# Row tiles of the first four experts: 32-row tiles (four abreast) replaced by 64-row tiles (two abreast)

## The reference

```python
logits = einsum('btd,de->bte', x, w_router)
top_val, top_idx = top_k(logits, 2)
gate = sum(one_hot(top_idx, 8) * softmax(top_val)[..., None], -2)
for e in range(8):
    out = out + gate[..., e:e+1] * swiglu(x, w_gu[e], w_down[e], 3584)
# swiglu: h = x @ w_gu;  (silu(h[..., :3584]) * h[..., 3584:]) @ w_down
```

## Time and profile before

| | us |
|---|---|
| median of the runs | 1730.22 |
| the profiled execution | 1730.22 |
| its span, first to last instruction | 1728.6 |
| TensorE busy, matmuls | 1625.6 |
| VectorE, ScalarE busy | 1041.6, 785.5 |
| DMA over the span | 460.65 MB, mean 266 GB/s |
| mean granted TensorE clock, share of full speed | 0.969 |

### The profile page before, as it was taken

The page is one execution under the profiler, slowest core; times in us unless marked ns, Lnnn a source line. Parts: engine busy times, 40 slices in busy tenths (PEclk is TensorE's granted clock), DMA queues, the critical chain, the costliest instruction groups (busy, mean ns, idle before and its releaser), DMA issues.

```text
span 1728.6 us, 27022 instructions
## 1 busy us (share of the span) xinstructions
PE 1625.6 (94%) x10366; PEld 1242.1 (72%) x10366; DVE 1041.6 (60%) x1356; ACT 785.5 (45%) x949; POOL 103.2 (6%) x187
## 2 busy tenths in 40 slices
PE   8999999999999999999899989787899999999897
PEld 6997899998976666865344535454688888888685
DVE  4998755446745554573213313231788888888797
ACT  4645543325533222342213312221677777777575
POOL 0000000000030541020000000000000000000300
PEclk9999999999998999999999999887999999999999
DMA  8773365442340441039999999999999999999992
GB/s 231 241 217 94 111 168 147 152 142 85 128 138 7 141 136 56 2 143 410 404 397 404 404 406 399 404 403 388 410 405 366 392 376 358 400 371 366 391 372 94
DMA packets 229947, 460.65 MB, mean 266 GB/s; under 512 B 24565, under 2 KB 120468, under 8 KB 229825
## 3 DMA queue, kind: packets, MB, share of 16 engines
q1 hardware_dynamic: 217246, 426.81, 67.5%
q10 hardware_dynamic: 5587, 17.16, 2.8%
q0 software_dynamic: 7008, 15.25, 2.7%
HBM read 440.86 MB, written 18.76 MB: 266 GB/s over the span
## 4 chain that ended last, share of the span: by engine, by line
PE 76%; DMA 9%; DVE 6%; ACT 5%; issue 2%; SPq 1%; POOL 0%; POOLq 0%; ACTq 0%; DVEq 0%
PE ps L2646 9%; PE ps L2802 8%; PE ps L2803 8%; PE ps L2804 8%; PE ps L2117 7%; PE ps L2119 7%; PE ps L2118 7%; DMA raw<-in_moe_w_gu 6%; PE ps L2199 3%; PE ps L2639 3%; PE ps L2640 2%; PE ps L2641 2%; PE ps L2488 2%; DMA raw<-in_moe_w_down 2%; PE ps L2451 2%
## 5 line engine op out<-in xcount | busy, mean ns | idle before, releaser
L1968 DVE TENSOR_TENSOR w_lo<-raw,w_hi 128x2048 fp32r<-128x2048 f32 x168 | 383.7, 2291 | 63.0 <-ACT w_hi L1275 62.1
L1275 ACT ACTIVATE w_hi<-raw 128x2048 fp32r<-128x2048 f32 x168 | 322.4, 1920 | 135.5 <-PE ps L2804 119.5
L1974 DVE TENSOR_TENSOR w_lo<-raw,w_hi 128x2048 fp32r<-128x2048 f32 x42 | 96.3, 2292 | 229.0 <-ACT w_hi L1282 229.0
L2117 PE MATMUL ps<-x_hi,w_hi 128*128 128x304 f32 x672 | 207.9, 309 | 2.2 <-DVE x_lo L1520 1.6
L2119 PE MATMUL ps<-x_lo,w_hi 128*128 128x304 f32 x672 | 202.8, 302 | 0.0
L2118 PE MATMUL ps<-x_hi,w_lo 128*128 128x304 f32 x672 | 202.0, 301 | 0.0
L2802 PE MATMUL ps<-w_hi,g_hi 128*128 128x512 f32 x448 | 177.7, 397 | 11.7 <-DVE w_lo L1968 11.7
L1410 DVE TENSOR_TENSOR w_lo<-raw,w_hi 128x2048 fp32r<-128x2048 f32 (+4 forms) x129 | 135.5, 1096 | 69.7 <-ACT w_hi L1002 69.5
L2803 PE MATMUL ps<-w_lo,g_hi 128*128 128x512 f32 x448 | 176.1, 393 | 0.0
L2804 PE MATMUL ps<-w_hi,g_lo 128*128 128x512 f32 x448 | 176.1, 393 | 0.0
L2646 PE MATMUL ps<-raw,g_s 128*32 128x128 f32 (+3 forms) x1920 | 161.1, 377 | 8.4 <-DMA raw<-in_moe_w_gu 8.4
(11 more groups left out here) (460 smaller groups left out, 2594.3 us busy)
## 6 DMA issues: line engine op xcount, KB each, us to landing
raw<-in_moe_w_gu SPq DMA_DIRECT2D x224, 1024.0 KB, 9.8
raw<-in_moe_w_down SPq DMA_DIRECT2D x112, 1024.0 KB, 9.2
raw<-in_ffn_w_gu SPq DMA_DIRECT2D x44, 512.0 KB, 5.1
raw<-in_conv_w_in SPq DMA_DIRECT2D x16, 512.0 KB, 7.8
raw<-in_ffn_w_down SPq DMA_DIRECT2D x16, 512.0 KB, 4.0
kvn<-in_cache_ckv POOLq DMA_DIRECT2D x64, 128.0 KB, 3.4
kvn<-in_cache_ckv SPq DMA_DIRECT2D x64, 128.0 KB, 2.8
rows_in<-zrow ACTq DMA_DIRECT2D x13, 512.0 KB, 3.7
```

The lines of the kernel that those rows point to most:

```text
L1275: nc.scalar.activation(w_hi[:, u % SPLIT], raw[:, u % RAW], ACT.Copy).then_inc(hi_done, 1)
L1968: V.tensor_tensor(w_lo[:, u % SPLIT], raw[:, u % RAW], w_hi[:, u % SPLIT].bitcast(F32), ALU.subtract).then_inc(lo_done, 1)
L1974: V.tensor_tensor(w_lo[:, n % F_SPLIT], first_raw(k), w_hi[:, n % F_SPLIT].bitcast(F32), ALU.subtract).then_inc(lo_done, 1)
L2117: nc.tensor.matmul(out, hi, xh, start=start, stop=False, skip_group_check=True)
```

## The change

C and H's further rows get 64 rows each, as A and B have: every plain product has two tiles. The table of rows goes away, and `HALF` (64) stands everywhere. With it go these sizes: a tile of C and H has twice the columns, C's and H's turns have more transposes (4 instead of 2 for a step of C, 2 instead of 1 for H's further rows), ScalarE and VectorE work on twice the width there, and the gather has 384 columns instead of 320. The routing arithmetic is simpler by one instruction, one of the DMAs that clear rows at the start falls away, and POOL stores C's and H's rows with 2 DMAs each instead of 4. H's limit is 192 tokens instead of 160 and C's 64 instead of 32 before an expert needs another job.

```diff
-ROWS = {"A": HALF, "B": HALF, "C": HALF // 2, "H": HALF // 2}
-TILES = {x: SLOTS // n for x, n in ROWS.items()}
-PLAIN = sum(ROWS.values())
-PLACES = SLOTS + PLAIN
+PLACES = SLOTS + FIRST_JOBS * HALF
...
-    hT_x = mo("hT_x", [P, SLOTS])
+    hT_x = mo("hT_x", [P, 2, SLOTS])
...
-    g_s = gx("g_s", [P, DC, PLAIN])
-    sgx = gx("sgx", [P, SLOTS])
+    g_s = gx("g_s", [P, FIRST_JOBS, DC, HALF])
+    sgx = gx("sgx", [P, 256])
...
-            for a in range(TILES[x]):
-                pool.dma_start(rows_out[r0:r0 + n, w * a:w * a + w], y_s[x][n * a:n * a + n]).then_inc(f_st, 16)
+            for a in range(2):
+                pool.dma_start(rows_out[r0:r0 + HALF, 512 * a:512 * a + 512], y_s[x][HALF * a:HALF * a + HALF]).then_inc(f_st, 16)
...
-        def plain_tiles(x, bank, n, rows, w, c0, start, stop):
-            for a in range(TILES[x]):
-                m = nc.tensor.matmul(ps[ROWS[x] * a:ROWS[x] * a + ROWS[x], bank, 0:n], rows, w[:, c0 + n * a:c0 + n * a + n],
+        def plain_pair(out, x, w, start, stop):
+            for a in range(2):
+                m = nc.tensor.matmul(out(a), x, w(a), start=start, stop=stop, skip_group_check=True)
...
-                m = nc.tensor.transpose(ps[:, 3, 0:P], hhx[:], ident[:])
+                for c in range(2):
+                    m = nc.tensor.transpose(ps[:, 3, P * c:P * c + P], hhx[:, P * c:P * c + P], ident[:])
...
-                    plain_tiles("H", 1 if kind == "gate" else 3, SLOTS, token_rows("H", c), w, 512 * q, c == 0, c == DC - 1)
+                    plain_pair(half_rows(1 if kind == "gate" else 3, 256), g_s[:, len(SMALL), c], columns(w, 512 * q, 256), c == 0, c == DC - 1)
```

More of the change, by code:

```diff
@@ L419, in build @@
     ADD_AFTER = {12: (0,), 19: (1,), 25: (2,), JOB_UNITS - 2: (3, 4, 5)}
-    y_s = {x: xt[:, i % 3, 512 * (i // 3):512 * (i // 3) + D // TILES[x]] for i, x in enumerate(FIRST_ROWS)}
+    y_s = {x: xt[:, i % 3, 512 * (i // 3):512 * (i // 3) + 512] for i, x in enumerate(FIRST_ROWS)}
     stat = place("stat", A0 + 4 * KB, [P, 3, 4])
@@ L955, in _ @@
             pool.wait_ge(f_fl, FLUSHED[x] + 1)
[L956 to L958 removed]
+            r0 = SLOTS + HALF * FIRST_ROWS.index(x)
+            for a in range(2):
+                pool.dma_start(rows_out[r0:r0 + HALF, 512 * a:512 * a + 512], y_s[x][HALF * a:HALF * a + HALF]).then_inc(f_st, 16)
         nc.gpsimd.iota(slot_no[:], pattern=[[1, SLOTS]], base=0, channel_multiplier=0,
                        allow_small_or_imprecise_dtypes=True).then_inc(slot_made, 1)
[L961 removed]
+        pool.wait_ge(f_st, 2 * FIRST_JOBS * 16)
         pool.wait_ge(last_dve, 3 + 1)
@@ L1322, in _ @@
                 act.wait_ge(unit_used, U_MOE + e + 1)
-                nc.scalar.activation(y_s[x], ps[:, 6 if x == "H" else 7, 0:D // TILES[x]], ACT.Copy).then_inc(f_fl, 1)
+                nc.scalar.activation(y_s[x], ps[:, 6 if x == "H" else 7, :], ACT.Copy).then_inc(f_fl, 1)
             for ahead in (2, 3) if k == 0 else (3,):
@@ L1888, in _ @@
         counts = ps[:, 4, 3 * NEXP:4 * NEXP]
-        key, rank_e, heavy, light, fewer, over, more, plain, dyn, first_row, limit_, shift = [ex[:, i] for i in range(12)]
+        key, rank_e, heavy, light, sign, over, more, plain, dyn, first_row, limit_, shift = [ex[:, i] for i in range(12)]
         square, by_first, tokens = [P, NEXP, NEXP], [P, FIRST_JOBS, NEXP], [P, 3, NEXP]
@@ L1897, in _ @@
         mark(V.tensor_tensor(picked[:], picked[:], eidx[:].unsqueeze(1).broadcast_to(by_first), ALU.mult))
-        chain(V.scalar_tensor_tensor(out=fewer, in0=light, scalar=-float(HALF / ROWS["H"]), in1=heavy, op0=ALU.mult, op1=ALU.add))
+        chain(V.tensor_tensor(sign, heavy, light, ALU.subtract))
         mark(V.reduce_sum(first_f[:], picked[:], AX))
-        chain(V.scalar_tensor_tensor(out=fewer, in0=rank_e, scalar=float(NEXP - 1), in1=fewer, op0=ALU.is_equal, op1=ALU.subtract))
+        mark(V.scalar_tensor_tensor(out=over, in0=sign, scalar=-float(HALF), in1=counts, op0=ALU.mult, op1=ALU.add))
+        chain(V.tensor_scalar(plain, sign, 0.0, None, ALU.is_equal))
         V.tensor_copy(first_i[:], first_f[:]).then_inc(ranked, 1)
-        mark(V.scalar_tensor_tensor(out=over, in0=fewer, scalar=float(ROWS["H"]), in1=counts, op0=ALU.mult, op1=ALU.add))
-        chain(V.tensor_scalar(plain, fewer, 0.0, None, ALU.is_equal))
         mark(V.tensor_scalar(more, over, float(2 * SLOTS), None, ALU.is_gt))
         mark(V.scalar_tensor_tensor(out=first_row, in0=rank_e, scalar=-float(NEXP - len(SMALL)), in1=light, op0=ALU.add, op1=ALU.mult))
-        chain(V.tensor_scalar(limit_, fewer, -float(ROWS["H"]), float(SLOTS), ALU.mult, ALU.add))
+        chain(V.tensor_scalar(limit_, sign, float(HALF), float(SLOTS), ALU.mult, ALU.add))
         mark(V.scalar_tensor_tensor(out=jobs[:], in0=over, scalar=float(SLOTS), in1=more, op0=ALU.is_gt, op1=ALU.add))
-        mark(V.scalar_tensor_tensor(out=first_row, in0=heavy, scalar=FIRST_ROW["H"] / HALF, in1=first_row, op0=ALU.mult, op1=ALU.add))
+        mark(V.scalar_tensor_tensor(out=first_row, in0=heavy, scalar=float(len(SMALL)), in1=first_row, op0=ALU.mult, op1=ALU.add))
         chain(V.scalar_tensor_tensor(out=key, in0=plain, scalar=float(4 * T), in1=limit_, op0=ALU.mult, op1=ALU.add))
@@ L1959, in gathered_lower @@
             of = ps[:, GATHER_LO[c % 3]]
-            V.tensor_copy(g_lo[:, c], of[:, PLAIN:PLACES])
+            V.tensor_copy(g_lo[:, c], of[:, FIRST_JOBS * HALF:PLACES])
             v.wait_ge(f_gh, c + 1)
-            V.tensor_tensor(g_s[:, c], of[:, 0:PLAIN], g_s[:, c], ALU.add).then_inc(f_gl, 1)
+            V.tensor_tensor(g_s[:, :, c], of[:, 0:FIRST_JOBS * HALF].rearrange("p (x n) -> p x n", x=FIRST_JOBS), g_s[:, :, c], ALU.add).then_inc(f_gl, 1)
         def split_moe(k, j):
@@ L2686, in _, with half_rows, columns @@
         gather(3)
-        def token_rows(x, c):
-            return g_s[:, c, FIRST_ROW[x]:FIRST_ROW[x] + ROWS[x]]
+        def half_rows(bank, n):
+            return lambda a: ps[HALF * a:HALF * a + HALF, bank, 0:n]
+        def columns(w, c0, n):
+            return lambda a: w[:, c0 + n * a:c0 + n * a + n]
         def turn_first(x, s):
@@ L2696, in turn_first @@
                     nc.tensor.transpose(ps[:, 2, P * c:P * c + P], hh[:, P * c:P * c + P], ident[:])
-                m = nc.tensor.transpose(ps[:, 3, 0:P], hhx[:], ident[:])
+                for c in range(2):
+                    m = nc.tensor.transpose(ps[:, 3, P * c:P * c + P], hhx[:, P * c:P * c + P], ident[:])
             else:
                 pe.wait_ge(f_hp, SMALL_N[x, s] + 1)
-                for c in range(narrow(x, s) // P):
+                for c in range(narrow(s) // P):
                     m = nc.tensor.transpose(ps[:, 2, P * c:P * c + P], hh_p[:, P * c:P * c + P], ident[:])
@@ L2710, in large_unit @@
                     c = 2 * part + q
-                    plain_tiles("H", 6, D // TILES["H"], hT_x[:, ROWS["H"] * c:ROWS["H"] * c + ROWS["H"]], w, WIDE * q,
-                                s == 0 and c == 0, s == 2 * STEPS - 2 and c == 3)
+                    at = HALF * (c // 2)
+                    plain_pair(half_rows(6, 512), hT_x[:, c % 2, at:at + HALF], columns(w, WIDE * q, 512),
+                               s == 0 and c == 0, s == 2 * STEPS - 2 and c == 3)
                 else:
@@ L2735, in small_unit @@
                     c = 2 * part + q
-                    a, at = divmod(c, narrow(x, s) // P)
-                    m = plain_tiles(x, 7, D // TILES[x], hT_s[:, at, ROWS[x] * a:ROWS[x] * a + ROWS[x]], w, WIDE * q,
-                                    s == 0 and c == 0, s == STEPS - 1 and c == 4 * n - 1)
+                    at = HALF * (c // (2 * n))
+                    m = plain_pair(half_rows(7, 512), hT_s[:, c % (2 * n), at:at + HALF], columns(w, WIDE * q, 512),
+                                   s == 0 and c == 0, s == STEPS - 1 and c == 4 * n - 1)
             else:
@@ L2741, in small_unit @@
                     c = (4 // n) * part + q
-                    m = plain_tiles(x, 0 if kind == "gate" else 2, narrow(x, s), token_rows(x, c), w, 512 * n * q, c == 0, c == DC - 1)
+                    m = plain_pair(half_rows(0 if kind == "gate" else 2, 256 * n), g_s[:, SMALL.index(x), c], columns(w, 512 * n * q, 256 * n),
+                                   c == 0, c == DC - 1)
             return m
```

31 lines of the change are left out of this document (14 added, 17 removed).

## The result

The changed kernel takes 1752.88 us, median of 4 runs (1751.49 to 1755.90), against 1730.06 (1727.85 to 1733.55) for the kernel before in the same comparison: a ratio of 1.0141, 95% interval 1.0127 to 1.0155. It is slower by 22.8 us. 1743 was forecast, with a range to 1751; the direction was right, the size was not. The profiled execution took 1749.95 us, 2.9 less than the median, the least of all executions of this kernel on record; its span is 1748.3 us, 19.7 longer than before, and 19.6 of it stand at the loop's first matmul. So a time read from the traces shows some 3 us less than the medians do.

What follows compares the result with a forecast made beforehand. Weight arrival bound the first four experts; TensorE would take over, 70.6 us added against 60 of slack. The loop would start at 1234 instead of 1220, plus 14, less 1 of gains: 1743 us, range 1733 to 1751.

Steps and rivals of the forecast that it cites:

- end of unit 160: Where the six places of the last units begin, ahead of the loop; forecast to move from about 1198.5 to 1212.5 us.
- work, with the turns' own waits: TensorE's work up to the end of unit 160: 368 us before plus 70.6 added, 438.6 us.
- further waits: TensorE's remaining wait for weights up to the end of unit 160, all at unit 52: 1.4 us.
- from there to the loop: From the end of unit 160 to the loop's start: DMA's path, not the changed work, 21.4 us as before.
- small gains: Unpriced gains, no passage between two tile shapes and a clock that falls less: 1 us taken off.
- Prices of a unit of C, of H's plain part: TensorE time: a unit of C gains 0.87 us over 0.865; H's plain part goes from 1.01 to 1.87.
- 5 of the 18 have no unit to cover the multiplication and take some 1.0 more: Turns up to unit 160: 0.8 us each, five uncovered ones some 1.0 more, 19 us together.
- Later TensorE is behind the arrivals everywhere, so nothing else waits: After unit 52, weights arrive before TensorE needs them, at units 97 and 122 by some 3 and 5 us.
- The wait at unit 52: H's gate after a long run of small units: weights at about 918.5, TensorE at 917.1, 1.4 us of wait.
- Slack as one sum of 60 us: TensorE's work of 368 us in 427.5 before the change leaves 60 us, set against 70.6 added.
- two bounds that add up: Rival: late places idle DMA, then TensorE waits for late weights; 1 to 2 us more per round, 1750 to 1756; chance 0.14.
- The rivals of the other side: Added work hides in the slack, 1731 to 1733, chance 0.10; or full clock makes it faster, 1727, chance 0.04.

Runs made afterwards that it cites:

- a_light: Changed kernel with the weight DMAs of the small experts' units from unit 16 on cut to half their columns: 1729.82 us, ratio 1.0002.
- a_turn: Changed kernel with VectorE's multiplication of hidden rows put ahead of the split of H's next unit at units 26, 98, 122: 1740.57 us, ratio 1.0079.
- h_only: Changed kernel with C back in 32-row tiles, four abreast, the gather keeping 384 columns: 1746.30 us, ratio 1.0095.
- h_turn: Changed kernel with C back in 32-row tiles and the three multiplications put ahead of the split: 1737.56 us, ratio 1.0042.
- b_turn: Kernel before the change, with the same three multiplications put ahead of the split: 1729.81 us, ratio 1.0007.

## Why the prediction was wrong

By its own steps, at the end of unit 160:

| step | forecast | measured |
|---|---|---|
| start of unit 0 | 772.5 | 770.5 |
| work, with the turns' own waits | 438.6 | 432.4 (a_light) |
| further waits | 1.4 | 16.1 |
| end of unit 160 | 1212.5 | 1219.0 |
| from there to the loop | 21.4 | 20.5 |
| loop's first matmul | 1234 | 1239.5 |

The loop is 5.5 us later than forecast. The median missed by 9.9: 1 of it was taken off for small gains, and some 3 lie between the profiled execution and the median.

- *What bounds the kernel, and that TensorE takes over*: right. The loop's rounds did not change, and what the loop starts late by, the end is late by.
- *Prices of a unit of C, of H's plain part*: right to 0.06 us. The sum was 6 us too high. Rows account for some 5: the 0.1 us of the passage from 64-row to 32-row tiles, seen at 21 places, is in the 438.6; a gather group takes 0.91 us and not 1.00; H's plain part in a down unit takes 1.81 and not 1.87; and each small unit was taken some 0.015 too dear. Unit 0 was taken 2 us too late: the first gather matmul starts at 761.77 instead of 763.45, and why was not tested. These two errors hid a part of the other by luck: with them right, the forecast would have been some 1735 and further off.
- *"5 of the 18 have no unit to cover the multiplication and take some 1.0 more"*: this is the step that failed. Two of the five (H's first and third step) do wait 1.1. The other three, A1, B2 and C0, stand ahead of a unit of H and wait in VectorE's queue for that unit: 5.62, 5.51 and 2.49 us, with a slow start behind the first two. Beyond the 2.4 us that they stand in a_light, that is 14.3 of the 16.1 us. The trace of before had it: unit 97 starts at 1027.33 and its turn at 1034.87.

```profile
1027.33 1.94 PE L2646 MATMUL ps<-raw,g_s 128*64 128x512 f32 x8 [0.66 <-DMA raw<-in_moe_w_gu]
1034.87 1.11 PE L2701 MATMUL ps<-ident,hh_p 128*128 128x128 f32 x4 [5.60 <-DVE hh_p L2004]
```

  I read the 7.5 us as part of the 60 us of slack, weights that come late, and took them away with it. But the arrival that the queue waits for moves with TensorE. Unit 26 (its DMA begun at 826.62 before and at 831.80 after) landed at 841.60 and at 844.76, 3.2 us later, and the up unit ahead of A1's turn started 3.2 us later too (838.92, 842.09). At B2 both are some 10 us later (unit 98 landed at 1029.98 and then at 1040.06), and the wait is again 5.5. At C0 TensorE is some 15 us later and unit 122 only 11.5 (1094.51, 1105.99), and there the wait did shrink, from 6.06 to 2.49. a_turn shows what the three cost: 12.3 us by the medians, 10.4 in the traces.
- *"Later TensorE is behind the arrivals everywhere, so nothing else waits"*: wrong in the same way. It compared arrivals as they were before, shifted by 4 us. But DMA can only be as early as places come free: unit 98 landed at 1040.06, not at some 1034.
- *The wait at unit 52*: 1.4 us forecast, 1.4 measured (from its start, 917.43, to the next unit's, 923.64, are 6.21 us against 4.82). That it agrees is in part luck: the wait for `w_lo` is 1.05 of it, 0.20 is the next unit's wait for the turned rows, and both TensorE and the weights came some 2 us later than forecast.
- *Slack as one sum of 60 us*: h_only shows that it isn't one. The time that DMA loses in the first three quarters isn't made good by TensorE's idle time in the last. The rival "two bounds that add up" had a part of this mechanism, late places, and the time, 1750 to 1756, with a chance of 0.14. That its time fits is in part luck, since the queued turns, over half of the cost, were not in it; its own argument against itself, that a swing of 5 us is small against 21 us of places, left out their standstill, which comes on top of the swing.
- *The rivals of the other side*: a unit of C costs double (1.715 against 0.865), and the work did not hide. The clock was full from 1120 to 1220, as foreseen, and fell at two of the turns; no gain came of it.

Of the 22.8 us, a_turn accounts for 12.3. What remains with the turns moved is 11.2 against the kernel before of that comparison, and splits by kernels into 8.0 for H alone (h_turn) and 3 for C on top of it. TensorE's work alone doesn't account for it: with light DMAs (a_light) the changed kernel's loop starts at 1219.4, where the kernel before has 1219.96. In h_turn it is the late start of the DMA stream (in the kernel after unit 9 is issued at 787.53 instead of 785.77) and the thin stretch from 900 to 1000 us, 3.8 and 7.2 us at 402 GB/s, less 2.5 won elsewhere. Which wait makes that second stretch thin, the alternation in H's steps or the turn and unit 52 within it, stays open.

## What to carry to other kernels

Before counting idle time as slack, ask of each wait what it hangs on, and whether that moves when the engine falls behind. Here the data did: its DMA was issued when the engine freed a place, so the two largest waits in the queue, for another unit's work, stayed at 5.5 us with TensorE 3 and 10 us later. Such a wait is free while another engine or DMA is the bound (b_turn), and becomes a cost when its own engine is (a_turn). Slack of one engine also couldn't be pooled over the stretch: what DMA lost early for want of a place was not made good later. Where a kernel alternates work by a fixed order, look for short work for the critical engine that stands behind long work waiting for an arrival, and put it ahead. It cost nothing here, and in the kernel before with 7 places it halved the loss.

## What the hardware showed that was not expected

Four units of A ahead of H's plain part take 7.02 us where that part has 32-row tiles, and 6.92 (879.24 to 886.16) where it has 64-row tiles as they do. Behind the standstills of 5.62 and 5.51 us the plain part took 3.15 and 2.79 us, at a mean granted clock of 0.56 and 0.62; behind the one of 2.49 us the clock was 1.00 and the part took 1.88. And one place of 1 MB fewer, out of eight, costs 14.5 us in a kernel whose DMA share is 1.03 with eight.
